# Eight adaLN units of the second layer: read in the merge through one ring slot and summed by VectorE, instead of in the projection by TensorE

## The reference

```
c_act = silu(c)
# first block (one layer)
mod_l = split(silu(c) @ ada_w[0] + ada_b[0], 6)
zl = modulate(rmsnorm(x), mod_l[0], mod_l[1]) @ w_in + b_in       # the projection
x = x + mod_l[2] * merge(hyena(zl), fnet(zl), mlstm(zl), gates(zl)) @ w_out
x = x + mod_l[5] * hier_moe(modulate(rmsnorm(x), mod_l[3], mod_l[4]))
# second block: two layers; layer 0 with a dense FFN, layer 1 with 8 experts
mod = c_act2 @ w_ada_2[layer] + b_ada_2[layer]
x = x + gt1 * hybrid_mixer(rms_norm(x) * (1 + sc1) + sh1)
x = x + gt2 * ffn_or_moe(rms_norm(x) * (1 + sc2) + sh2)
```

## Time and profile before

| | |
|---|---|
| median of 3 runs | 1922.56 us (1921.06 to 1926.6) |
| the profiled execution, its own time | 1927.68 us |
| its span, first to last instruction | 1925.8 us |
| PE busy | 1842.1 us, 96% of the span |
| DVE busy | 688.6 us, 36% |
| ACT busy | 312.8 us, 16% |
| DMA | 538.84 MB, mean 280 GB/s |
| mean granted PE clock | 0.989 of full speed |

### The profile page before, as it was taken

The page is one execution under the profiler, slowest core; times in us unless marked ns, Lnnn a source line. Parts: engine busy times, 40 slices in busy tenths (PEclk is TensorE's granted clock), DMA queues, the critical chain, the costliest instruction groups (busy, mean ns, idle before and its releaser), DMA issues.

```text
span 1925.8 us, 39004 instructions
## 1 busy us (share of the span) xinstructions
PE 1842.1 (96%) x17396; PEld 1080.7 (56%) x17396; DVE 688.6 (36%) x1670; ACT 312.8 (16%) x729; POOL 26.5 (1%) x41
## 2 busy tenths in 40 slices
PE   6999989999898899999999999999999999999997
PEld 2654767886777555577676555443444444343444
DVE  3766772622433665432323553311110111111023
ACT  3211121001233324200001242100000010000001
POOL 0100000000000000000000000100000000000000
PEclk9999999999999999999999999999999999999999
DMA  9967743353699443467675323799999999999995
GB/s 359 341 244 272 272 153 118 131 178 119 263 401 388 164 141 123 148 235 256 236 242 190 131 91 128 294 402 420 409 419 409 416 409 405 420 412 415 410 413 217
DMA packets 156047, 538.84 MB, mean 280 GB/s; under 512 B 10016, under 2 KB 34944, under 8 KB 121712
## 3 DMA queue, kind: packets, MB, share of 16 engines
q1 hardware_dynamic: 149360, 509.15, 68.7%
q0 software_dynamic: 3728, 17.58, 2.6%
q10 hardware_dynamic: 2784, 9.53, 1.3%
HBM read 527.18 MB, written 12.19 MB: 280 GB/s over the span
## 4 chain that ended last, share of the span: by engine, by line
PE 87%; DVE 6%; DMA 2%; issue 1%; DVEq 1%; ACT 1%; SPq 0%; POOL 0%; ACTq 0%; POOLq 0%
PE ps L1279 24%; PE ps L1315 12%; PE ps L1225 8%; PE ps L1513 8%; PE ps L1089 4%; PE ps L1207 4%; PE ps L1237 4%; PE ps L892 4%; PE ps L1291 3%; PE ps L1104 2%; PE ps L1333 2%; PE ps L757 2%; PE ps L699 1%; PE ps L1302 1%; DMA ring<-in_ada_w 1%
## 5 line engine op out<-in xcount | busy, mean ns | idle before, releaser
L1279 PE MATMUL ps<-ring,arena 128*32 128x512 f32 (+1 forms) x4608 | 459.1, 557 | 0.0
L1279 PEld LDWEIGHTS ps<-ring,arena 128*32 128x32 f32 x4608 | 148.9, 110 | 294.0 <-issue 288.2
L1315 PE MATMUL ps<-ring,arena 128*32 128x256 f32 x4224 | 232.2, 379 | 0.1
L1315 PEld LDWEIGHTS ps<-ring,arena 128*32 128x32 f32 x4224 | 139.4, 110 | 96.9 <-issue 12.4
L2862 DVE TENSOR_TENSOR arena<-arena,ps 128x256 f32<-128x256 f32 (+1 forms) x72 | 27.0, 375 | 390.8 <-ACT arena L1965 390.8
L1513 PE MATMUL ps<-ring,hT 128*128 128x512 f32 (+1 forms) x384 | 154.9, 554 | 1.1 <-DVE hT L2214 1.1
L1225 PE MATMUL ps<-hT,ring 128*128 128x256 f32 x704 | 153.8, 379 | 0.7 <-DVE hT L2214 0.7
L1225 PEld LDWEIGHTS ps<-hT,ring 128*128 128x128 f32 x704 | 133.6, 190 | 23.4 <-issue 5.7
L1513 PEld LDWEIGHTS ps<-ring,hT 128*128 128x128 f32 x384 | 69.1, 190 | 68.7 <-issue 66.8
L2758 DVE TENSOR_SCALAR arena<-ps,ga,mod 128x128 f32<-128x128 f32 (+1 forms) x64 | 20.8, 389 | 197.5 <-PE ps L1330 118.1
L1089 PE MATMUL ps<-hT,ring 128*128 128x256 f32 x384 | 86.6, 385 | 3.9 <-DMA ring<-in_w_branch 3.9
(11 more groups left out here) (426 smaller groups left out, 1805.8 us busy)
## 6 DMA issues: line engine op xcount, KB each, us to landing
ring<-in_gate_up SPq DMA_DIRECT2D x160, 1024.0 KB, 14.2
ring<-in_down SPq DMA_DIRECT2D x104, 1024.0 KB, 15.2
ring<-in_gate_up_last SPq DMA_DIRECT2D x64, 768.0 KB, 13.9
ring<-in_w_ada SPq DMA_DIRECT2D x48, 768.0 KB, 6.1
ring<-in_w_in SPq DMA_DIRECT2D x36, 768.0 KB, 7.8
ring<-in_ada_w SPq DMA_DIRECT2D x24, 768.0 KB, 7.8
ring<-in_w_ada SPq DMA_DIRECT2D x24, 512.0 KB, 7.1
ring<-in_w_in SPq DMA_DIRECT2D x12, 1024.0 KB, 7.5
```

The costliest lines, as they stand in the source:

```text
L1279: last = mm(ps[32 * q:32 * q + 32, base + t_, 0:2 * n], src[:, k, 32 * t_:32 * t_ + 32], w[:, q], start=k == 0, stop=k == KD - 1)
L1315: last = mm(ps[32 * q:32 * q + 32, bank + t_ // 2, (t_ % 2) * 256:(t_ % 2 + 1) * 256], rows[:, t_, o:o + 32], cells[:, cell, r * D + q * 2 ...
```

## The change

Units 15, 16, 18, 20, 21, 22 and 23 (PE's until now) and unit 19 (DVE's, in the projection) are in the new list `MOVED`. Their loads leave the projection and stand among the loads of the merge. Each goes to ring slot 2, and waits until DVE has summed the one before it. The six merge units use slots 0 and 1 alone, and the two `w_out` units slots 2 and 0. DVE sums the moved units at eight places of its merge order into the arena. PE adds over the partitions with 128 matmuls of one column (`moved_columns`) between the halves of `turn("x2")`, in the place of the six `busy` matmuls. DVE copies the result behind `router1()`. `LAST_STRIP` becomes unit 9: the ACT copy and the 16 closing matmuls stand in pass kc.

The new order of SP's loads behind the projection is: merge 0, merge 1, units 15, 16, 18, 19, merge 2, unit 20, merge 3, merge 4, units 21, 22, merge 5, unit 23, out1 0, out1 1.

```diff
-SUMMED = (10, 11, 12, 13, 14, 17, 19)
-LAST_STRIP = 2 * NA - 1
+SUMMED = (10, 11, 12, 13, 14, 17)
+MOVED = (15, 16, 18, 19, 20, 21, 22, 23)
+N_SUMS = len(SUMMED) + len(MOVED)
+LAST_STRIP = 9
...
-    return loads + rest, releases + rest
+    late = [ADA_UNITS[i] for i in MOVED]
+    queue = rest[0:2] + late[0:4] + rest[2:3] + late[4:5] + rest[3:5] + late[5:7] + rest[5:6] + late[7:8] + rest[6:8]
+    return loads + queue, releases + rest
...
-        if name in ("merge", "out1"):
-            s = wide % NS
-            wide, full[s] = wide + 1, full[s] + 1
+        if name in ("merge", "out1") or (name, j) in MOVED_UNITS:
+            s = j % 2 if name == "merge" else 2 - 2 * j if name == "out1" else 2
+            wide, full[s] = s + 1, full[s] + 1
...
+        if (name, j) in MOVED_UNITS:
+            SUMS_BEFORE[name, j] = MOVED_UNITS.index((name, j))
+            continue
+        if name == "out1" and j == 0:
+            SUMS_BEFORE[name, j] = len(MOVED)
...
             def strip_rows(i):
 
-                if i in SUMMED:
+                if i in SUMMED or i in MOVED:
                     return
...
+            def moved_columns():
+
+                pe.wait_ge(sem("ada_sum"), N_SUMS)
+                for n, (_, u) in enumerate(MOVED_UNITS):
+                    for m in range(4):
+                        last = mm_strips(ps[:, 1, 4 * u + m:4 * u + m + 1], region(R_KC + 512 * n + m * P, P), const("ones")[:, 0:1],
+                                         start=True, stop=True)
+                last.then_inc(sem("moved_mm"), 1)
...
-            turn("x2", fill=(0, 6))
+            turn("x2", between=moved_columns)
...
             z_in("kc", 0)
             spectrum_in(0)
+            strip_in(LAST_STRIP)
             z_in("kc", 1)
...
-                if h == 3:
-                    strip_in(LAST_STRIP)
...
-                if j in (0, 2):
-                    ada_sum(*ADA_UNITS[19 if j else 17])
+                if j == 0:
+                    ada_sum(*ADA_UNITS[17])
...
             conv_hy(6, 7, 10)
+            ada_sum(*MOVED_UNITS[0])
+            ada_sum(*MOVED_UNITS[1])
             merge(0)
+            ada_sum(*MOVED_UNITS[2])
             hyena_products(0)
             merge(1)
             merge(2)
+            ada_sum(*MOVED_UNITS[3])
             hyena_out(0)
...
             merge(4)
             merge(5)
+            ada_sum(*MOVED_UNITS[4])
             hyena_out(1)
...
             merge(6)
+            ada_sum(*MOVED_UNITS[5])
             merge(7)
             dve.wait_ge(sem("gaterow_mm"), 1)
             v.tensor_copy(grow[:, 0, :], all_ps[:, 2048:3072]).then_inc(sem("gaterow_in"), 1)
+            ada_sum(*MOVED_UNITS[6])
             merge(8)
...
+            ada_sum(*MOVED_UNITS[7])
             merge(9)
...
             router1()
+            dve.wait_ge(sem("moved_mm"), 1)
+            v.tensor_copy(modn[:, 12:20], ps[:, 1, 12:20])
+            v.tensor_copy(modn[:, 24:48], ps[:, 1, 24:48])
             dve.wait_ge(sem("late_in"), 32)
```

More of the change, by code:

```diff
@@ L210, in unit_order @@
     for p, name in enumerate(PASSES):
-        a, b = ADA_UNITS[4 + 2 * p:6 + 2 * p]
+        a, b = ([ADA_UNITS[i]] if i not in MOVED else [] for i in (4 + 2 * p, 5 + 2 * p))
         unit = ("in1", IN1_UNIT[name])
-        loads = loads + ([unit] if unit not in loads else []) + [a, b]
+        loads = loads + ([unit] if unit not in loads else []) + a + b
         held = [unit] if name not in ("k", "v") else []
         early = 5 + 2 * p not in SUMMED and 5 + 2 * p < LAST_STRIP
-        releases = releases + [a] + ([b] + held if early else held + [b])
+        releases = releases + a + (b + held if early else held + b)
     rest = [("merge", j) for j in range(6)] + [("out1", j) for j in range(2)]
-    return loads + rest, releases + rest
+    late = [ADA_UNITS[i] for i in MOVED]
+    queue = rest[0:2] + late[0:4] + rest[2:3] + late[4:5] + rest[3:5] + late[5:7] + rest[5:6] + late[7:8] + rest[6:8]
+    return loads + queue, releases + rest
+MOVED_UNITS = [ADA_UNITS[i] for i in MOVED]
 LOADS, RELEASES = unit_order()
@@ L2173, in ada_sum @@
                 s, _, n = PLAN[name][0][u]
-                of, ready = (ring, full) if name == "ada2" else (quads, quad_full)
+                moved = (name, u) in MOVED_UNITS
+                of, ready = (ring, full) if name == "ada2" or moved else (quads, quad_full)
                 dve.wait_ge(ready[s], DMA3 * n)
@@ L2465, in _ @@
             head_out(7)
-            dve.wait_ge(used, USED["ada1"][NA - 1])
+            dve.wait_ge(used, USED["ada1"][5])
             v.tensor_copy(mod[:, 16:48], ps[:, 3, 32:64])
```

10 lines of the change are left out of this document (8 added, 2 removed).

## The result

The changed kernel took 1929.95 us (median of 17 runs, 1924.55 to 1933.9), the kernel before, run beside it, 1922.37 us (17 runs, 1917.69 to 1927.83). The ratio is 1.0031 [1.0021, 1.004] (with its 95% interval): 6 us slower, 4 to 8 by the interval, and 7.6 by the two medians, where 11.7 us faster was forecast. The profiled execution took 1926.91 us, its span 1925.1 us.

The account below looks back on a forecast made before the run. PE was taken to bound the kernel nearly everywhere, with DVE's chain of like length from 178 to 290 us. 9.0 (projection) + 3.9 (merge unit 0) - 1.2 (merge) = 11.7 us off 1922.56 gave 1911 us, range 1904 to 1918.

Parts of the forecast that it names:

- The clock: 0, at most 2.0: Around fnet_columns and gates_of(0): the low clock's cost of 1.95 us stays, so gain 0, at most 2.0 us.
- the passes vh to fn: Projection: six units' rows leave PE and one sum leaves DVE, so fnet_columns starts 9.0 us earlier.
- the second rival: Half the gain, 1914 to 1920 us: the projection's new gaps drop the clock and late landings add 1 to 3; chance 0.12.
- The load of merge unit 0: Ahead of gates_of(0): its ring slot is free earlier, so PE's 3.90 us wait for this load goes whole.
- the wait of 1.2 us for merge unit 5: Late merge: the load lands at 23.7 us behind branch_of(6)'s end, PE wants it at 22.5, so PE waits 1.2.
- bound 0 to 4: Merge waits: 0 if shared landings are 1 us quicker, 4 us if POOL's 3 MB of fills halve the rate for one round.
- The prediction's own sign of being wrong: Merge: a moved unit landing more than 2 us later than 7.9, or a changed length behind 510 us.
- the slack of 0 to 1.3: Merge unit 2 ahead of gates_of(4): lands at 339.4, wanted at 340.1, no wait; with the clock up, wait 1.3 us.
- the single slot becomes the bound: Rival, merge: longer rounds push three chained rounds ahead of gates_of(4) and merge unit 5; slower, up to 1937 us; chance 0.06.
- Behind the merge: 0, at most +1.5: x2 turn: 2.6 us of one-column matmuls hidden in place of 2.75 us of busy; up to 1.5 us if the clock falls.
- The shift is carried through: Behind 510 us: the experts' loads are keyed to PE's releases, so the earlier start reaches the end.
- given back downstream: Rival, behind 510 us: the experts' loads absorb the gain, no change, 1920 to 1925 us; chance 0.06.

Follow-up runs that it names:

- e15: e10 with its cover cut to 6, 4, 4 and 7 busy matmuls for 9, 7, 7 and 12; 1914.15 us, 0.9956 of the kernel before.
- e12: The kernel before, unchanged, measured and profiled a second time; 1923.31 us in that profile, ratio 0.9999.
- e1: The changed kernel once more, unchanged; 1927.44 us, 1.0034 of the kernel before.
- e8: Changed kernel with reordered loads and sums, 80 short matmuls ahead of out_proj, 48 between its halves, 6 busy in the x2 turn; 1919.86 us, 0.9992.
- e6: Changed kernel with the moved loads and sums, but without the 128 one-column matmuls and two copies, 6 busy in the x2 turn; 1926.83 us, 1.0009.
- e9: Changed kernel with the load and sum order of e8, its 128 one-column matmuls left in the x2 turn; 1925.69 us, 1.0009.
- e3: Changed kernel with the 128 one-column matmuls moved between out_proj's halves and 6 busy back in the x2 turn; 1926.69 us, 1.0013.
- e2: Kernel before with only 128 one-column matmuls on constants replacing the 6 busy in the x2 turn; 1928.54 us, 1.0035.
- e7: Kernel before plus 128 one-column matmuls in eight groups of 16 between the merge's last branches, busy kept; 1926.4 us, 1.0019.
- e10: e8 with 9, 7, 7 and 12 busy matmuls ahead of gate_columns, ml_values(4), ml_values(6) and fnet_columns; 1919.84 us, 0.9987 of the kernel before.
- e13: e10 again, unchanged; 1918.52 us, 0.9972 of the kernel before.
- e16: e15 with the sum of unit 20 behind hyena_products(1) instead of ahead of it; 1919.84 us, 0.9983 of the kernel before.
- e11: Kernel before with 26 more busy matmuls in the x2 turn, a delay alone; 1937.54 us, 1.0091.
- e14: e10 with 14 more busy matmuls in the x2 turn; 1919.15 us, 0.9995 of the kernel before.

## Why the prediction was wrong

**Ahead of the merge: the mechanism was right, the step "The clock: 0, at most 2.0" was mis-sized.** The forecast said 12.9 us at `gates_of(0)`. With PE kept occupied (e15) it is 235.8 - 223.1 = 12.7 us: the step sums of the passes vh to fn, the vanished wait for merge unit 0 and the slack of DVE are borne out. Step by step, from e12 to e15: 5.3 us at `ml_values(4)` for 5.5 forecast, 7.2 at `ml_values(6)` for 7.4, 8.7 at `fnet_columns` for 9.0. In the changed kernel it is 7.0. What failed is that I looked for the clock's cost at one place, behind the merge unit's wait, and took the new gaps of about 2.2 us as free because DVE is the longer chain there. They can each drop the clock (0.50 at 234 to 237 and 258 to 261), and the slow matmuls stand ahead of `row_maxima`, for which DVE waits: the slowdown goes into DVE's chain too. It is not always the same gap: in e1 the clock was 1.00 behind the one ahead of `ml_values(4)` (1.80 us for the 14 matmuls) and 0.52 behind the 3.22 us ahead of `fnet_columns` (6.55 us for the 16), where the profile after shows 1.00 behind 3.44 us. Against e15, e1 has lost 1.8 us by `ml_values(0)`, 3.4 by `ml_values(7)` and 5.7 by `gates_of(0)`; e8 4.2, 7.5 and 9.8. This was the second rival, at 0.12: the mechanism it named is shown, by e8 against e15. Its "against", that DVE is the longer chain around those gaps, is what did not hold.

The Trainium skill, "TensorE: Matmul & The Clock Gate", section "A second HAM failure mode: psum-queue depth-cycling", states that an engine which idles briefly but often between groups of matmuls can lose its clock as well as one that waits long. The rows above agree, with 0.50 behind gaps of 2.2 us, though not at every such gap. Its pages on the rates, weighed ahead, changed nothing: the windows show up to 403 GB/s again, and a sum took 0.49 + 5.71 us on DVE, as counted. The 0.9 us that the prediction gives for 5.2 MB at the page's rate is a slip: 5.2 MB take 13.2 us at 393 GB/s and 14.5 at 358, 1.3 more.

**The load of merge unit 0: right.** The wait of 3.90 us is gone in every run of the changed kernel.

**The merge: the wait of 1.2 us for merge unit 5 was 2.6 to 8.4.** `hyena_inverse(0)` and units 3 and 4 had no wait, as said. For unit 5 the rounds were counted with 7.9 us for a load. In the profile after, unit 21 was issued at 387.95 and DVE could start its sum at 400.18, after 12.2; from the end of `branch_of(6)` unit 22 was issued 9.2 us later, not 7.8, and merge unit 5 landed at 25.3, not 23.7. In e6 unit 21 took 18 us. The prediction named the cause (POOL's 3 MB of fills, bound 0 to 4), gave it too narrow a bound, and left out that a wait of PE also brings the clock down behind it (0.57 at 431 to 438 us in e6). The prediction's own sign of being wrong, a landing more than 2 us later than 7.9, was there. That merge unit 2 was late by 2.72 us in one profile and not in the other fits the slack of 0 to 1.3 that was read there. That the queue's order is the cause is shown by e9: with it changed, there is no wait for `w_branch`, and 4 us are back. The rival "the single slot becomes the bound" had the direction of the result, and late rounds as its mechanism, but not the place: its three chained rounds ahead of `gates_of(4)` ended in a wait of 2.7 us at most.

**"Behind the merge: 0, at most +1.5" failed**: it was 5.2 us. The 2.6 us of short matmuls were sized rightly (1.99 + 0.70, and 2.31 in e3), and the cover of 2.75 us was there to be replaced. What was left out is that PE can stand still with its operands there. After 202 to 219 records of 9 ns it stopped for 4.85 to 5.97 us in all four profiles that had the burst in the turn (after, e1, e2, e9). No stop of that length came in those that had the same matmuls elsewhere (e3, e7, e8, e10, e13 to e16); e3 and e8 show one of 1.23 and 0.91 us just behind their short matmuls.

What the stop waits for can be read from the DMA queue that the profile calls "instruction". Its row in the window 482 to 484 of the kernel after:

```profile
q8 instruction: 1, 0.02, 3.0%
```

This is one packet of 16 KB. None came from 458 to 482 us, this one ended at 483.6, and PE went on at 485.15. In e1, e2 and e9 too the stop holds just one such packet, the first for 24 us or more, and PE goes on 1.4 us, 1.4 us and 1.5 us behind its end. It is so everywhere: in the 18 profiles PE has 115 idle times over 0.6 us marked `issue` between 440 and 650 us, and each ends 1.2 to 1.6 us after the end of a 16 KB packet of this queue. That PE waits there for its next instructions is thus as good as shown. Why the packet comes late is not: in e3, at a DMA share of 0.01, it began 2.6 us behind the start of the short matmuls, in the four bursts, at 0.95 to 1.00, it began 4.4 to 5.5 us behind. That it queues behind the weights' packets fits, but no run varied the DMA load at one place.

**"The shift is carried through": right, against appearances.** e11 carried 10.4 us of delay as 15.4 (2.2 of it lost ahead of the delay), and e15 carried 10.2 us of gain at moe1's start as 10.7 at its end. The rival "given back downstream" has nothing for it in e15; e10, e13 and e14 have moe1 at 133.1, 131.7 and 129.8 us, e15 126.8. Part of the difference is the same kind of stop: in every profile, before too, PE stands 10.0 to 14.6 us of moe1 idle with `issue` as the mark, and the longer moe1 is, the more of it there is (10.2 and 10.8 us in before and e12, 12.4 in after and e1, 13.7, 13.1, 12.5 and 11.3 in e10, e13, e14 and e15; a correlation of 0.88 over the 18). Why its amount differs stays open. Over all profiles moe1 lasted 126.6 to 128.7 us in ten of the eleven executions that entered pass q late (131.7 in e13) and 129.5 to 133.6 in the seven that entered it early. How much of this is the start and how much the kernel is not settled: the two kernels profiled once early and once late show 1.0 us (after 129.6, e1 128.6) and 1.4 us (e10 133.1, e13 131.7) for some 4 us of start.

**The base.** One row was read short: the 0.64 us for 32 short matmuls hold 59 of their 64 records, so 128 take nearer 2.8 us than 2.6, against the 2.3 to 2.8 measured. The difference was rightly taken off the median and not off the profiled time. But steps were counted against a profile that was itself slow by 3.4 us ahead of `out_proj` (1.7 of them at a clock of 0.65 behind `gate_columns`, 180 to 184 us, where e12 shows 1.00); by e12 the starts forecast for after would have been earlier.

**The sum.** Predicted -12.9 + 1.2 + 0 = -11.7. Measured in stages: -7.0, + 4.0, + 5.2, + 1.8 in moe1 and + 0.6 behind = +4.7, by the ratio +6 [4, 8]. The 0.75%, 14 us, between after and e15 split, undone one after the other, into 4 for the order of the loads (after to e9), 3 for the place of the columns (e9 to e8) and 7 for the cover of the gaps (e8 to e15); each share has an error of about 3 us.

## What to carry to other kernels

Where work is taken off PE and another engine then ends the wait, the gap is not free: give it its length in cover matmuls, no more (e10's excess cost 3.3 us at `gates_of(0)`, e15's fit brought 7 in the time), and count what the slow matmuls behind it do to the engine that waits for them. A shared queue with a chain of load, sum, release in it holds up every load behind it, so put the load with a due time ahead of the round that has none, and start the rounds that must stand ahead of it as early as their sums allow. Do not put hundreds of the shortest instructions in a row where the DMA engines are full. And where PE idles with `issue` as the mark, look for a packet of the instruction queue just ahead of its end.
